# Three borders between blocks: the next block's input as root times (y by both weights) plus a prepared product of x

## What is computed

```
def _rmsnorm(x, g):
    xf = x.astype(jnp.float32)
    y = xf * lax.rsqrt(jnp.mean(xf * xf, axis=-1, keepdims=True) + EPS)
    return (y * g.astype(jnp.float32)).astype(x.dtype)

def _swiglu(x, wg, wu, wd):
    return (jax.nn.silu(x @ wg) * (x @ wu)) @ wd

for l in range(DEPTH):                       # first stack, DEPTH = 2
    h = _swiglu(_rmsnorm(x, g[0]), ...)      # feed-forward, hidden width 2816
    x = x + 0.5 * _rmsnorm(h, g[1])
    h = mixer(_rmsnorm(x, g[2]), ...)        # l = 0: convolution + window attention; l = 1: forgetting attention
    x = x + _rmsnorm(h, g[3])
    h = _swiglu(_rmsnorm(x, g[4]), ...)
    x = x + 0.5 * _rmsnorm(h, g[5])
```

## Time and profile before

| | |
|---|---|
| median of 3 runs | 1751.82 us (1751.68 to 1752.38) |
| the profiled execution | 1750.6 us |
| its span in the trace | 1748.8 us |
| mean granted TensorE clock | 0.974 of full speed |
| PE busy | 1646.7 us, 94% |
| DVE busy | 1060.6 us, 61% |
| ACT busy | 830.7 us, 47% |

### The profile page before, as it was taken

The page is one execution under the profiler, slowest core; times in us unless marked ns, Lnnn a source line. Parts: engine busy times, 40 slices in busy tenths (PEclk is TensorE's granted clock), DMA queues, the critical chain, the costliest instruction groups (busy, mean ns, idle before and its releaser), DMA issues.

```text
span 1748.8 us, 24334 instructions
## 1 busy us (share of the span) xinstructions
PE 1646.7 (94%) x9424; PEld 1423.7 (81%) x9424; DVE 1060.6 (61%) x1331; ACT 830.7 (47%) x1018; POOL 41.8 (2%) x80
## 2 busy tenths in 40 slices
PE   6999895899999999899999998988999989999998
PEld 5888794688888888798788887967888879878887
DVE  4566778666667666645566666465566654555665
ACT  4445544454445454535454454454544444544444
POOL 7000000000000000000000000000000000000000
PEclk9999997999999999999999998999999999999999
DMA  7565541356555555453265654425655555046552
GB/s 249 178 208 175 168 145 49 100 189 200 182 194 185 190 178 192 146 168 121 73 207 171 208 174 160 142 97 168 192 193 177 183 198 163 1 129 208 173 187 97
DMA packets 197255, 284.89 MB, mean 163 GB/s; under 512 B 8816, under 2 KB 149136, under 8 KB 197184
## 3 DMA queue, kind: packets, MB, share of 16 engines
q1 hardware_dynamic: 193488, 271.09, 47.5%
q0 software_dynamic: 3552, 12.28, 2.1%
q10 hardware_dynamic: 144, 0.52, 0.1%
HBM read 282.81 MB, written 1.05 MB: 162 GB/s over the span
## 4 chain that ended last, share of the span: by engine, by line
PE 86%; DVE 8%; ACT 4%; issue 1%; DMA 0%; DVEq 0%; POOL 0%; POOLq 0%; ACTq 0%
PE ps L1366 49%; PE ps L1437 21%; PE ps L1439 10%; DVE mx L1137 2%; DVE w_lo L947 1%; PE ps L1601 1%; PE ps L1386 1%; DVE xt L1006 1%; PE ps L1657 1%; DVE xn L969 1%; ACT shared L834 1%; PE ps L1645 1%; ACT xt L660 1%; DVE x_res L973 0%; DMA gain<-in_norm_g_dram 0%
## 5 line engine op out<-in xcount | busy, mean ns | idle before, releaser
L947 DVE TENSOR_TENSOR w_lo<-raw,w_hi 128x2048 fp32r<-128x2048 f32 x257 | 587.9, 2291 | 417.2 <-ACT w_hi L616 417.2
L616 ACT CAST w_hi<-raw 128x2048 fp32r<-128x2048 f32 x257 | 489.0, 1905 | 139.9 <-PE ps L1366 99.8
L1437 PE MATMUL ps<-xt,w_hi 128*128 128x512 f32 x1536 | 544.1, 398 | 0.0
L1439 PE MATMUL ps<-xt,w_lo 128*128 128x256 f32 x1536 | 431.2, 281 | 0.0
L1437 PEld LDWEIGHTS ps<-xt,w_hi 128*128 128x128 f32 x1536 | 288.6, 188 | 71.3
L1366 PE MATMUL ps<-xt,w_hi 128*128 128x256 f32 x1616 | 296.2, 285 | 4.5 <-issue 2.4
L1439 PEld LDWEIGHTS ps<-xt,w_lo 128*128 128x128 f32 x1536 | 290.0, 189 | 1.9
L1366 PE MATMUL ps<-w_hi,xt 128*128 128x512 f32 (+1 forms) x736 | 239.5, 408 | 28.5 <-DVE xt L1006 12.4
L1366 PEld LDWEIGHTS ps<-xt,w_hi 128*128 128x128 f32 x1616 | 255.2, 194 | 6.2 <-issue 2.6
L1366 PE MATMUL ps<-xt,w_lo 128*128 128x256 f32 x808 | 230.0, 285 | 0.0
L1366 PE MATMUL ps<-w_hi,ht_hi 128*128 128x512 f32 x528 | 207.2, 392 | 0.0
(11 more groups left out here) (213 smaller groups left out, 1298.6 us busy)
## 6 DMA issues: line engine op xcount, KB each, us to landing
raw<-in_ffn_w_gate_dram SPq DMA_DIRECT2D x132, 512.0 KB, 4.0
raw<-in_ffn_w_up_dram SPq DMA_DIRECT2D x132, 512.0 KB, 4.9
raw<-in_ffn_w_down_dram SPq DMA_DIRECT2D x132, 512.0 KB, 4.2
raw<-in_fox_w_in_dram SPq DMA_DIRECT2D x24, 512.0 KB, 4.5
raw<-in_a_w_in_dram SPq DMA_DIRECT2D x24, 512.0 KB, 4.5
raw<-in_w_kv_dram SPq DMA_DIRECT2D x16, 512.0 KB, 5.0
raw<-in_ab_w_in_dram SPq DMA_DIRECT2D x14, 512.0 KB, 4.8
gain<-in_norm_g_dram POOLq DMA_DIRECT2D x12, 512.0 KB, 4.1
```

Of the source, the lines that this page charges most:

```text
L616: nc.scalar.copy(w_hi[slot][:, :], raw[slot][:, :]).then_inc(hi_made, 1)
L947: nc.vector.tensor_tensor(w_lo[slot][:, :], raw[slot][:, :], w_hi[slot][:, :].bitcast(F32), ALU.subtract).then_inc(lo_made, 1)
L1437: nc.tensor.matmul(ps[:, GU_LOOP + b, :], w_hi[slot][:, cols], xt[:, kb, :], start=kb == 0, stop=False)
L1439: ins = nc.tensor.matmul(ps[:, GU_LOOP + b, 0:S], w_lo[slot][:, cols], xt_hi[:, kb, :], start=False, stop=kb == KB - 1)
```

## The change

At the three borders the input of the next block is made in another form. Before, x + root * (y * g_post) is made first and then multiplied by g_pre. After, it is root * (y * gg) + xg, where gg = g_post * g_pre and xg = x * g_pre are prepared before y is complete (`fuse_ready`: three operations of 128x1024 on DVE, in the convolution mixer's spare memory `mx`). The product y * gg waits only for ACT's square of y, not for the root. The residual x itself is updated after the fourth `xt_lo` (`added_y`). PE's transposes of group 0 move ahead of PE's last piece of work on y.

More of the change, by code:

```diff
@@ L240, in program @@
         sinks = sb("sinks", [P, 8])
+        xg = mx[:, 0:8, :].rearrange("p a b -> p (a b)").rearrange("p (t n) -> p t n", t=T)
+        gg = mx[:, 8:12, :].rearrange("p a b -> p (a b)")
         prob = [shared[:, i * 3 * P:(i + 1) * 3 * P] for i in range(3)]
@@ L393, in program @@
         n_z_ln = []
+        n_y_squared = []
         def group_place(s, g):
@@ L640, in post_square @@
                                           accum_out=pssq[:, t:t + 1]))
+                n_y_squared.append(n_step)
                 eps = epst if s["scale"] == 1.0 else eps4t
@@ L1355, in _ @@
                     lo_upto(s["piece"] + 4)
+                    if s.get("fuse"):
+                        fuse_ready(s["fuse"])
         @block.tensor
@@ L1507, in ffn @@
                 down_block(q + 1, 0, 1, 0)
+                if s.get("fuse"):
+                    turn(s["fuse"], 0)
                 down_block(q + 1, 1, 1, 0, stop=True).then_inc(piece_used, 1)
```

## The result

The changed kernel takes **1788.38 us** (median of 4 runs, 1787.36 to 1789.53) against 1751.75 us before (median of 4); the ratio is 1.0212 with a 95% interval of 1.020 to 1.0225. It is 37 us slower. The forecast was 1783 us, range 1768 to 1795.

A forecast was written before the change was run, and what follows sets the result against it. PE, busy for 94% of the span, was taken to bound the kernel. 1750.6 us profiled + 22.1 of waits + 9 of clock = 1781.7; with the profiled execution 1.2 us under the median, forecast 1783 us, range 1768 to 1795.

The forecast's parts named there:

- What bounds the kernel: Whole kernel: only PE's standing still counts; its waits at the three borders hold at most 7.3 us.
- The second border: Walk through PE, ACT and DVE at this border: PE reaches `gate_up(p + 2)` 6.95 us later than before.
- piece p+1: Before group 1's product PE waits for its low part: 5.0 us at the second border, 4.9 at the first.
- p+2: Before `gate_up(p + 2)` PE waits 3.5 us for the low part of this piece.
- The update of x: Behind groups 2 and 3: ACT's square of x holds back `lo(p+2)`, 3.5 us; then no wait or a few tenths.
- only the first loss is real: Rival: `lo(p+2)` comes in time at the borders, so PE pays 11.7 us: 1763.5 us; chance 0.05.
- What costs nothing: `fuse_ready`'s three added DVE operations (1.15 us each, 3.4 in all) and the shifted loads of POOL and SP: nothing.
- Sum of the waits: Over the three borders: 6.95 + 2 x 7.6 = 22.1 us.
- The clock: Lower PE clock after the new waits: 3 us a border, 9 us in all, between 0 and 18.
- the place in the earlier trace: After a 3.21 us wait, clock 0.53 for 6 us and 0.59 from 748 to 756 us: 6.1 us, the bound per border.

The follow-up runs named there:

- `fused_best`: `three_early` with group 2's transposes, its low part, tile 0's x-update products and the low part of piece p+2 placed differently: 1746.65 us, ratio 0.9974.
- Experiment 1: The changed kernel with the low part of piece p+1 moved back between the low parts of groups 0 and 1 on DVE: 1763.42 us, ratio 1.0067.
- Experiment 2: The changed kernel with piece p+2 made ahead of the update of x: 1787.01 us, ratio 1.0203.
- the filler: The changed kernel with 10 and 7 unread products on PE ahead of its waits for pieces p+1 and p+2: 1771.95 us, ratio 1.0126.
- My first filler: The changed kernel with 20 and 13 unread products on PE ahead of its waits for pieces p+1 and p+2: 1789.65 us, ratio 1.0224.
- `three_early`: The changed kernel with pieces p+1 and p+2 made earlier and piece p+3 made inside the border too: 1751.55 us, ratio 1.0009.

## Why the prediction was right

- **What bounds the kernel.** Right: only PE's waits counted. The 7.3 us that could be won at most was too high: the first and third border have waits of 1.64 us and not 2.44, so 5.7 us in all. `fused_best` removed 3.4 us of them and won 4.6.
- **The second border.** Forecast: 0.45 us for group 0's transposes, 5.0 us for piece p+1, group 2 covered by nothing, 3.5 us for p+2; in the trace 0.29, 4.98, 0.96 and 3.26. At the first border I gave 4.9 us for piece p+1; it was 4.96. Experiment 1 shows the cause of this wait: DVE's order, not the arithmetic.
- **The update of x.** The price was right; its description as piece p+2 standing behind the square of x was too narrow. Experiment 2 took the piece out of that place and the time stayed. Behind it the SiLU and piece p+3 are as late. I had them ready within a few tenths of PE's need, which held only because PE was already late by the wait for p+2: with that wait gone, 3.3 us stand at them. The rival "only the first loss is real" is out as well, for the second wait was there in full.
- **What costs nothing.** The prepared products: 1.0006. One of 128x1024 took 1.22 us, 1.14 to the next, where I took 1.15. At the first border DVE still had 0.44 us of idle time behind them.
- **Sum of the waits.** 22.1 forecast; 22 measured by the filler. The rows agree: 9.17, 9.49 and 9.39 us of waits at the three borders less 1.64, 2.44 and 1.64 make 22.3.
- **The clock.** The term that was mis-sized: 9 us (0 to 18) forecast, 15 measured, inside the bounds. Two things were wrong in it. I took half of what the place in the earlier trace rows paid, because of the cover that groups 2 and 3 have. But the low clock did not fall on groups 2 and 3. It fell on group 1's product and on `gate_up(p + 2)`, straight behind the waits, where nothing covers it: group 1's slow product delays the transposes, the update of x and piece p+2 with it. And I counted that place as one wait with two slow stretches. Its second stretch (748 to 756, 3.3 of the 6.1 us) has no wait ahead of it; from 743 to 749 PE was busy with products of only 16 columns and the clock fell in them:

```profile
743.50 0.37 PE L1366 MATMUL ps<-zw_hi,xt 128*128 128x16 f32 x2
...
747.52 0.41 PE L1366 MATMUL ps<-zw_hi,xt 128*128 128x16 f32 x2
...
749.28 1.20 PE L1366 MATMUL ps<-w_hi,xt 128*128 128x512 f32 x2
```

  What its one wait of 3.21 us cost is the row from 725 to 731, 2.8 us. Here each of the six long waits cost 1.4 to 2.8 us, so two such prices a border, uncovered, would have been the better term. Without the second stretch my upper bound would have been 3 x 2.8 = 8.4 us, and the 15 measured would lie above it: that the term stayed inside its bounds is luck. The Trainium skill ("TensorE: Matmul & The Clock Gate", Part 1) has the slow level as the default that activity releases; by that, work right behind a long pause is the work that pays, and the trace agrees (0.50 from 553 to 558 and from 569 to 575 us).

## What to carry to other kernels

When an operation chain is shortened on an engine that issues in order, look at what else its list carries for the engine that bounds the kernel: a piece of work moved behind a wait of its neighbour cost 25 us here, and the shorter chain, together with a better placement of the pieces around it, is worth 4.6. Removing a wait can show the same loss at the next consumer of the chain (p+2, then p+3, then the hidden tile), so follow the chain to its end before moving one product. And price each long wait on TensorE with the clock behind it: here 22 us of waiting (waits of 5.0 and 3.3 us) brought 15 us more, while waits of up to 1.7 us left the clock at 1.00.

## What the runs showed of the hardware that was not expected

- Products that nobody reads, put into waits, made the changed kernel 16 us faster (1788.4 to 1772.0 us; 15 us by the ratios to the kernel before), since the granted clock stayed at 1.00 at the borders.
- Products of 128x256 in plain f32 (the filler's operands) took 4.53 us for 10, 0.45 us each, with two records for each product in the trace ("x20"). The kernel's own products, of operands that it holds as f32r (the number format of the profile's `fp32r`), took 0.12 each (48 of 128x256 in 5.75 us, 546.40 to 552.15 before). My first filler was almost twice as long as the waits.
- A single wait of 3.2 us (experiment 1) still lowered the clock of its window (528 to 580 us: 0.97 against 1.00 in `three_early`, where the longest wait is 1.7 us). It cost less there than in the changed kernel: the 48 products behind it took 7.3 us (551.91 to 559.24) where they took 8.5.
- The clock also fell without a wait: in the kernel before, 0.59 from 748 to 756 us, behind 5 us of 16-column products in which PE was busy throughout.
